# Routing and the first expert in one program block: a shorter search round, ranks from bf16 products, first weights split early

## What is computed

```python
def expert_choice_moe(x2d, w_router, w_gate, w_up, w_down):
    n, D = x2d.shape
    cap = EC_CAPACITY_FACTOR * n // N_EXPERTS
    affinity = jax.nn.softmax((x2d @ w_router).astype(jnp.float32), axis=-1)
    gates, idx = lax.top_k(affinity.T, cap)
    xe = x2d[idx]
    h = jax.nn.silu(jnp.einsum('ecd,edf->ecf', xe, w_gate)) * jnp.einsum('ecd,edf->ecf', xe, w_up)
    ye = jnp.einsum('ecf,efd->ecd', h, w_down) * gates[..., None].astype(x2d.dtype)
    return jnp.zeros_like(x2d).at[idx.reshape(-1)].add(ye.reshape(-1, D))
```

## Time and profile before

| | |
|---|---|
| median of 3 runs | 3785.76 us (3784.28 to 3788.94) |
| profiled execution, its own time | 3786.3 us |
| its span in the trace | 3784.5 us |
| PE busy | 3483.8 us (92% of the span) |
| PEld busy | 2976.8 us (79%) |
| DVE busy | 2231.4 us (59%) |
| ACT busy | 1564.8 us (41%) |
| POOL busy | 824.0 us (22%) |

### The profile page before, as it was taken

The page is one execution under the profiler, slowest core; times in us unless marked ns, Lnnn a source line. Parts: engine busy times, 40 slices in busy tenths (PEclk is TensorE's granted clock), DMA queues, the critical chain, the costliest instruction groups (busy, mean ns, idle before and its releaser), DMA issues. The chain is left out here.

```text
span 3784.5 us, 51837 instructions
## 1 busy us (share of the span) xinstructions
PE 3483.8 (92%) x19069; PEld 2976.8 (79%) x19069; DVE 2231.4 (59%) x3959; ACT 1564.8 (41%) x2003; POOL 824.0 (22%) x403
## 2 busy tenths in 40 slices
PE   8999979996999999997999559999999999999991
PEld 6888878874777777775777459999999999999990
DVE  5444457766888888885555455555555555555545
ACT  2111144443677767765222123333333333333335
POOL 0000000004677767774111001111111111111100
PEclk9999989997999999998999669999999999999995
DMA  3111155655222233202333035555555555555536
GB/s 121 63 61 61 54 180 205 213 210 131 44 41 46 55 56 55 55 8 90 128 133 128 28 125 162 165 172 168 161 165 172 168 161 161 161 169 171 170 111 247
DMA packets 341115, 470.64 MB, mean 124 GB/s; under 512 B 105472, under 2 KB 241408, under 8 KB 338304
## 3 DMA queue, kind: packets, MB, share of 16 engines
q1 hardware_dynamic: 329216, 427.10, 35.9%
q0 software_dynamic: 11776, 41.95, 5.3%
HBM read 352.91 MB, written 116.08 MB: 124 GB/s over the span
## 5 line engine op out<-in xcount | busy, mean ns | idle before, releaser
L63 PE MATMUL psum<-xeT_hi,w_hi 128*128 128x320 f32 x2048 | 635.5, 310 | 0.1
L65 PE MATMUL psum<-xeT_hi,w_lo 128*128 128x320 f32 x2048 | 633.8, 309 | 0.0
L64 PE MATMUL psum<-xeT_lo,w_hi 128*128 128x320 f32 x2048 | 633.7, 309 | 0.0
L1346 POOL TENSOR_TENSOR added<-added,p_hi 128x1024 f32<-128x1024 f32 x192 | 459.1, 2391 | 157.3 <-ACT p_hi L1300 156.6
L2027 ACT ACTIVATE w_hi<-w_raw 128x2048 fp32r<-128x2048 f32 x192 | 358.6, 1908 | 294.7 <-PE psum L65 199.5
L2105 DVE TENSOR_TENSOR w_lo<-w_raw,w_hi 128x2048 fp32r<-128x2048 f32 x192 | 432.3, 2286 | 39.4 <-ACT w_hi L2027 39.4
L63 PEld LDWEIGHTS psum<-xeT_hi,w_hi 128*128 128x128 f32 x2048 | 385.4, 188 | 1.1
L64 PEld LDWEIGHTS psum<-xeT_lo,w_hi 128*128 128x128 f32 x2048 | 385.4, 188 | 0.6
L65 PEld LDWEIGHTS psum<-xeT_hi,w_lo 128*128 128x128 f32 x2048 | 385.3, 188 | 0.0
L1382 DVE TENSOR_TENSOR p_lo<-psum,p_hi 128x1024 fp32r<-128x1024 f32 x272 | 332.6, 1223 | 89.3 <-ACT psum L1302 88.3
L1300 ACT ACTIVATE p_hi<-psum 128x1024 fp32r<-128x1024 f32 x272 | 279.3, 1027 | 227.0 <-PE psum L65 227.0
(11 more groups left out here) (335 smaller groups left out, 7142.5 us busy)
## 6 DMA issues: line engine op xcount, KB each, us to landing
w_raw<-in_w_gate SPq DMA_DIRECT2D x64, 1024.0 KB, 5.0
w_raw<-in_w_up SPq DMA_DIRECT2D x64, 1024.0 KB, 9.5
w_raw<-in_w_down SPq DMA_DIRECT2D x64, 1024.0 KB, 5.2
rec<-rec SPq DMA_DIRECT2D x20, 768.0 KB, 3.6
recb<-rec SPq DMA_DIRECT2D x20, 768.0 KB, 5.1
xa<-in_x SPq DMA_DIRECT2D x20, 512.0 KB, 4.4
xb<-in_x SPq DMA_DIRECT2D x20, 512.0 KB, 6.0
v_lo_hi<-v SPq DMA_DIRECT2D x16, 640.0 KB, 10.3
```

What stands on the lines that cost most here:

```text
L63: pe.matmul(out, a[0], b[0], start=first, stop=False)
L64: pe.matmul(out, a[0], b[1], start=False, stop=False)
L65: return pe.matmul(out, a[1], b[0], start=False, stop=last)
L1346: g.tensor_tensor(acc[:], so_far, p_hi[at % 4][:].bitcast(F32), ALU.add).then_inc(s["p_added"], 1)
```

## The change

`routing_phase` is emptied; its work stands at the start of `moe_phase`, in the same block as the experts. In detail:

- The affinities are laid out anew (`laid`, three blocks of 128 columns, of which each of the first two has 96 prompt and 32 sample columns, and the third 64 prompt columns and padding of -1), so that prompt and sample rows lie in different partitions of one tile. A search round has one comparison (128x384) and one product (`same` and `count` in fp32r, two columns).
- The update of `thr` stands behind the comparison. Behind it each round has one small piece of other work: in rounds 0 to 3 constants, in rounds 12 to 27 one sixteenth of the subtraction that makes `w_lo` of chunks 0 and 1.
- Ranks: `mask`, `tri` and `ones` are bf16, with one more tile slot behind each group. One product with `tri` and 20 accumulating products with `ones` for each of the two masks give the ranks and, in the added slots, the totals. The 18 steps and most of the six behind them are gone.
- SP issues the first four weight loads at the start of the block and waits for the gather of expert 0 (`gathered` >= 48) before the fifth. ACT rounds chunks 0 to 3 during the search. DVE makes `w_lo` of chunks 2 and 3 behind the turns of expert 0 instead of ahead of them.
- The eight turns of expert 0 use six banks (`FIRST_BANK`); only turns 6 and 7 wait for a bank.

```diff
@@ moe_phase, sync
                 for n in range(4):
                     sp.dma_start(shaped(raw[n], n), chunk_source(0, n)).then_inc(raw_in[n], 16)
+                sp.wait_ge(s["gathered"], 48)
                 with sp.Fori(0, E - 1) as e:
@@ moe_phase, tensor
+                def find_places():
+                    pe.wait_ge(s["aff_laid"], 1)
+                    for b in range(3):
+                        ins = pe.transpose(ps[:, 5, b * P:(b + 1) * P], laid[:, b, :], c.ident)
+                    ins.then_inc(s["aff_turned"], 1)
+                    for i in range(BITS):
+                        pe.wait_ge(s["compared"], i + 1)
+                        pe.matmul(ps[:, 0, 0:2], same[:], count[:], start=True, stop=True).then_inc(s["counted"], 1)
+                    pe.wait_ge(s["thr_spread"], 1)
+                    pe.transpose(ps[:, 7, 0:P], thr_wide[:].bitcast(F32), c.ident).then_inc(s["thr_turned"], 1)
+                    pe.wait_ge(s["masks_made"], 1)
+                    for m in range(2):
+                        pe.matmul(ps[:, 1 + m, 0:NTZ * E], tri[:], mask[:, m, :, :].rearrange("p t e -> p (t e)"),
+                                  start=True, stop=False, skip_group_check=True)
+                        for first, last in ((0, NTP), (NTP + 1, NT + 1)):
+                            for t in range(first, last):
+                                ins = pe.matmul(ranks(m)[:, t + 1:last + 1, :], ones[:],
+                                                bc(mask[:, m, t, :], 1, [P, last - t, E]), start=False,
+                                                stop=t == NT, skip_group_check=True)
+                        ins.then_inc(s["ranked"], 1)
@@ turn
-                    else:
+                    elif banks is None:
                         pe.wait_ge(s["xT_lo_made"], e * DK + (k - 1))
+                    elif k >= 6:
+                        pe.wait_ge(s["xT_lo_made"], k - 5)
@@ moe_phase, vector
+                    for i in range(BITS):
+                        bit = 1 << (BITS - 1 - i)
+                        v.wait_ge(s["candidate"], i + 1)
+                        v.tensor_scalar(above[:], affT[:], cand[:].bitcast(F32), None, ALU.is_ge, ALU.add,
+                                        accum_out=count[:, 0:1]).then_inc(s["compared"], 1)
+                        if i > 0:
+                            v.tensor_tensor(thr[:], thr[:], took[:], ALU.bitwise_or).then_inc(s["thr_taken"], 1)
+                        if PIECES_FROM <= i < PIECES_FROM + 2 * CH // PIECE:
+                            lo_piece(i - PIECES_FROM)
...
+                        v.wait_ge(s["counted"], i + 1)
+                        wait_from_one(v, s["thr_taken"], i)
+                        step(v.tensor_scalar(took[:], ps[:, 0, 0:1], float(CAP_P), float(bit), ALU.is_ge, ALU.mult))
+                        if i + 1 < BITS:
+                            v.scalar_tensor_tensor(out=cand[:], in0=took[:], scalar=bit >> 1, in1=thr[:],
+                                                   op0=ALU.bitwise_or, op1=ALU.bitwise_or).then_inc(s["candidate"], 1)
...
-                v.tensor_copy(iota[:], c.const[:, C_IOTA:C_IOTA + CAP_P]).then_inc(s["iota_made"], 1)
-                v.wait_ge(s["iota_made"], 1)
+                search()
+                find_places()
                 make_hots(0)
                 take_lists(0)
-                make_lo(0, 0)
+                for k in range(DK):
+                    take_turned(0, k, FIRST_BANK)
                 make_lo(0, 1)
-                for k in range(DK):
-                    take_turned(0, k)
                 experts(v, body)
```

More of the change, by code:

```diff
@@ L1833, in moe_phase @@
+    c.aff = aff
 def moe_phase(c, slot_no, vals):
@@ L1863, in moe_phase @@
         gate_next, gate, part = sb("gate_next", [P, 3]), sb("gate", [P, 3]), sb("gate_part", [P, 3])
+        thr, cand, took = (sb(n, [P, 1], I32) for n in ("thr", "cand", "took"))
+        laid = sb("aff_laid", [P, 3, P])
+        affT, above = sb("affT", [P, 3 * P]), sb("above", [P, 3 * P])
+        count = sb("count", [P, 2], F32R)
+        same, row = sb("same", [P, P], F32R), sb("same_row", [P, E])
+        thr_wide, thr_row = sb("thr_wide", [P, P], I32), sb("thr_row", [P, P])
+        full = sb("full", [P, 2, E])
+        ones, tri = sb("ones", [P, P], BF16), sb("tri", [P, P], BF16)
+        mask = sb("mask", [P, 2, NTZ, E], BF16)
+        places, t1, rank1 = (sb(n, [P, NTZ, E]) for n in ("places", "rt1", "rank1"))
+        left1, left2 = sb("left1", [P, NT, E]), sb("left2", [P, NT, E])
         raw_in = [c.sem(f"e_raw_in{r}") for r in range(4)]
@@ new lines, in find_places @@
+                def find_places():
+                    v.wait_ge(s["thr_turned"], 1)
+                    step(v.tensor_copy(thr_row[:], ps[:, 7, 0:P]))
+                    v.wait_ge(s["constants_set"], 1)
+                    for g, ts, zs in groups:
+                        shape = [P, ts.stop - ts.start, E]
+                        t = bc(thr_row[:, ROWS_P * g:ROWS_P * g + E], 1, shape)
+                        v.tensor_tensor(mask[:, 0, zs, :], affv[:, ts, :], t, ALU.is_gt)
+                        ins = v.tensor_tensor(mask[:, 1, zs, :], affv[:, ts, :], t, ALU.is_equal)
+                    ins.then_inc(s["masks_made"], 1)
+                    v.wait_ge(s["masks_made"], 1)
+                    v.wait_ge(s["ranked"], 1)
+                    totals = ps[:, 1, NTP * E:NTP * E + 10 * E].rearrange("p (g x) -> p g x", g=2)[:, :, 0:E]
+                    v.tensor_copy(full[:], totals)
+                    step(v.scalar_tensor_tensor(out=t1[:], in0=ranks(0), scalar=-BIG, in1=mask[:, 0, :, :],
+                                                op0=ALU.add, op1=ALU.mult))
+                    v.wait_ge(s["ranked"], 2)
+                    for g, ts, zs in groups:
+                        shape = [P, zs.stop - zs.start, E]
+                        ins = v.tensor_tensor(rank1[:, zs, :], ranks(1)[:, zs, :], bc(full[:, g, :], 1, shape), ALU.add)
+                    step(ins)
+                    for g, ts, zs in groups:
+                        ins = v.scalar_tensor_tensor(out=rank1[:, zs, :], in0=rank1[:, zs, :], scalar=-BIG,
+                                                     in1=mask[:, 1, zs, :], op0=ALU.add, op1=ALU.mult)
+                    step(ins)
+                    for g, ts, zs in groups:
+                        ins = v.scalar_tensor_tensor(out=places[:, zs, :], in0=t1[:, zs, :], scalar=BIG - 1.0,
+                                                     in1=rank1[:, zs, :], op0=ALU.add, op1=ALU.add)
+                    step(ins)
```

230 lines of the change are left out of this document (83 added, 147 removed).

## The result

The changed kernel took 3744.78 us (median of 4 runs, 3743.10 to 3746.98), the kernel before, run beside it, 3785.02 us (4 runs, 3783.93 to 3788.94). The ratio is 0.9892, with a 95% interval of 0.9875 to 0.9909: 40.2 us faster. 3745 us had been predicted. The profiled execution has a span of 3745.2 us, 39.3 less than before.

What follows compares the result with a forecast made beforehand. PE fills the span except a 119.1 us hole before the first expert matmul, a serial DVE-PE-DVE chain. Seven terms sum to -40.5 us, from 3786.3 to 3745.8, or 3745 us as median; forecast 3741 to 3750, range 3739 to 3754.

Steps and rivals of the forecast that it cites:

- What bounds the kernel: Claim that PE fills nearly all the span outside the hole, so the change is worth what it removes there.
- The hole: Stretch from the output phase's last step to the first expert matmul, without model matmuls: 119.1 us, forecast to become 78.6.
- Step 1, start: Output phase's last step to the search's first comparison: barrier, copies, transposes and ACT copy sum to 3.39 us, losing 1.6.
- Step 2, rounds: The 30 search rounds: 2.39 us each become 1.48, with pieces and `thr` hidden; 27.4 us gained.
- The first rival: Search rounds save less: fp32r product no faster, or pieces and waits delay `took`; with both, 8.1 us, 3753; chance 0.13.
- Step 3: Spreading the threshold after the search: same steps with 128 columns instead of 32 and 16; 0.1 us lost.
- Steps 4 and 5, ranks and boundary: Masks' end to `hot_p`: bf16 products and fewer DVE steps gain 8.1 us, removing barrier and `iota` gains 1.65.
- Step 6, gather: POOL's first gather to first turn: 12.26 us becomes 8.2 without weight loads or `w_lo` beside it; 4.0 us gained.
- the bound from above: Upper estimate of gather landing: third gather issued at 2.4 us at the latest, landing 6.9 later, 9.3 in all.
- The rival in which 12.26 stays: Gather bound by its own descriptors and latency, so its 12.26 us stays and the kernel takes 3749; chance 0.06.
- Step 7, turns: Expert 0's eight turns run at PE's own pace of 0.91 us: 8.36 us becomes 7.3, 1.05 gained.
- a rival's part: In expert 0's start, full clock from the first matmul saves 2.5 us; part of a more-gained rival, chance 0.06.

Runs made afterwards that it cites:

- experiment 1: Changed kernel with `same` and `count` in fp32 instead of fp32r: rounds of 1.69 us (+0.21), the search +6.0 us; 3745.47 us in one run.
- experiment 2: Changed kernel with the `w_lo` pieces taken out of the search and made whole beside the gather: first gather to first turn 12.49 us (+3.9).
- experiment 6: Changed kernel with the two `left` subtractions moved from POOL to DVE, in rounds 5 and 8: search 44.22 us (-1.1), the hole 77.9 us.
- experiment 8: Changed kernel with the fifth and sixth weight loads started together with the gather: gather to first turn 10.46 us (+1.9), the hole 81.4 us.
- experiment 3: Changed kernel with expert 0's eight turns on two PSUM banks instead of six: turns 7.95 us (+0.64), the hole 79.9 us.
- Experiment 7: Changed kernel with 44 unused bf16 products on PE between expert 0's list and its turns: turns 4.58 us (-2.7); 3739.79 us.

## Why the prediction was right, step by step

**What bounds the kernel.** Held. The hole shrank by 39.5 us, the total by 40.2, and neither what lies ahead of the hole nor what lies behind it changed by more than 0.8. The parts are what the forecast can be credited with. That the median came within 0.2 us of it is in part luck: the hole is 1.0 us short of the sum, the profiled execution took 3747.0 where the sum had 3745.8, and the runs themselves spread over 3.9 us.

**Step 1, start (forecast +1.6, measured +1.3).** The term was mis-sized. The barrier with the clearing left DVE idle for 1.02 us, not the 1.37 of its old place; copies with the small memset 0.54 (0.55 taken), transposes 1.00 (0.92), ACT with its hand-over 0.52 (0.55).

**Step 2, rounds (-27.4, measured -26.5).** The mechanism held part by part: 27 of 29 rounds are 1.47 or 1.48. The first rival's two conditions were both tried, and neither holds: fp32r does save a pass (experiment 1), and the pieces cost nothing (experiment 2). The 27.4 should read 27.3 (30 times 0.91). What the step had no term for is POOL's `left` subtractions, which hold `cand` in rounds 0 and 1 for 1.1 us (experiment 6). In the kernel before, the same two ran at 2118.48 and 2121.14, 0.9 us each, almost wholly while DVE waited for the products; one `cand` started beside them, 0.06 us ahead of the second one's end, and took its 0.16. The price of a round had been taken from a late one.

The Trainium skill ("SBUF — State Buffer", section "SBUF: two separate sides") says that GpSimd and a VectorE instruction with two inputs in SBUF want the same pair of ports (where the GpSimd instruction reads SBUF), that whoever starts first has it for the whole instruction, and that the other is blocked. The traces here agree where POOL subtracts and where it is the one that waits: `cand` (it reads `took` and `thr`) ends with POOL's instruction within 0.02 us, and POOL's gathers end 0.8 to 1.0 us behind the `w_lo` beside them. They don't agree that DVE waits for a gather: the `w_lo` that started while POOL's first gather ran took the same 2.29 us as the others.

**Step 3.** Held (+0.13).

**Steps 4 and 5, ranks and boundary (-9.75, measured -9.75).** Held; PE's part 4.7 us where 4.65 was taken, DVE's 1.8 where 1.85 was. The open price, wide bf16 products, is that of fp32r ones by the column: 5376 columns in 4.71 us at half clock. At the 0.82 ns a column of the earlier trace rows that leaves 0.3 for start and drain, and nothing for their number.

**Step 6, gather (-4.0, measured -3.7).** The total was right, the reason half right. I had put the slow gather down to full transfer engines alone. Before, POOL was done with its third instruction 6.44 us behind the first one's start, and is now after 3.63; from there to the first turn it was 5.82 and is 4.93. So 2.8 of the 3.7 us are POOL, held by DVE's `w_lo`, and 0.9 the transfers. The 0.9 is the weaker number: in the runs with nothing beside the gather, POOL's end to the first turn takes 4.6 to 5.4 us. Experiment 2 brings back the one cause (+3.9 on POOL, nothing behind it), experiment 8 the other (+1.9 behind POOL, nothing on it). As for the size, 8.56 instead of 8.2: the bound from above, 9.3, had two errors that went against each other. The third gather is issued later than taken (2.72 us behind the first, not 2.4 at the latest, since POOL is idle for 0.30 between two of them), and it lands sooner (5.8, not 6.9, which had been the least of 48 with loads or a held POOL around all of them). The middle of 9.3 and 6.9 is 8.1, and nothing but a choice between the bounds stood behind the 8.2, so that it came this close is luck. The rival in which 12.26 stays is out.

**Step 7, turns (-1.05, measured -1.05).** Held; 0.6 of it is the banks (experiment 3), and the other 0.4 fits the freed DVE. The two `w_lo` behind the turns cost nothing: expert 0 is full (89.89 of 90.5 us).

**The clock.** It had been taken as unchanged up to the first matmul, and was: 0.50 for 4.4 us into expert 0 (5.0 before). Experiment 7 shows what was priced as a rival's part: full clock from the start of the turns is worth 4.7 us, 2.0 of it in expert 0. The rival had put up to 2.5 us on the latter, and had no gain in the turns.

What is missing from the sum is thus 1.0 us of 40.5, 0.9 of it in the rounds.

## What to carry to other kernels

A serial search is a chain of hand-overs: price a round by its rows from start to start, fuse what shares a hand-over, and put other work only into the gap where its engine waits, with the gap's size beside the piece's. When an indirect gather on POOL or a small DVE step looks slow, look at what the other of the two engines runs at that time before blaming transfers; moving a long two-input DVE instruction out of the gather gained more here than freeing the transfer engines. Where PE waits with nothing to do ahead of a dense stretch, unused products in the wait can be worth their place: here 4.7 us in the two stretches behind one loop of 44.

## What the runs showed of the hardware that I had not expected

- DVE and POOL can hold each other. A 128x1 `SCALAR_TENSOR_TENSOR` of 0.16 us took 0.78 beside a 0.90-us POOL `TENSOR_TENSOR`; a POOL `DMA_INDIRECT` of 1.14 us took 5.13 beside 4.48 us of DVE `w_lo`. A `w_lo` that started beside a running `DMA_INDIRECT` was not held.
- The time at which the clock rises varies from run to run at the same instructions. At the start of expert 0 it came 4.4 and 3.7 us behind the first matmul in the two traces of the changed kernel, and 2.3 us (experiment 1) to 4.9 us (experiment 2) in the others that enter it at 0.50. In experiments 1, 2 and 6 it rose already within the ranks, where the second mask's 20 products took 1.40 us in experiment 1 instead of 2.17; the changed kernel's two traces have it at 0.50 there. That is 0.4 to 0.8 us of difference that no edit made. What decides it stays open.
- Transposes can run through at the high clock. The Trainium skill ("TensorE: Matmul & The Clock Gate", "Part 4: PE-mode transpose") says that the high clock does not engage for them. Experiment 7, where it was up before they began, has it at 1.00 through all 4.56 us of them, and there the measurement decides; the changed kernel has it at 0.50 through 7.3 us of them. Neither run shows whether transposes alone would raise it.
